# Value products of an attention in one session behind the last transposes, panel parts between the groups of transposes

## The reference, cut to what matters

```
s = einsum('bnqhgd,bnkhd->bnhgqk', qb, kw) * 64 ** -0.5      # 128 queries x 256 keys
s = where(valid, s, -inf)
m = maximum(max(s), sink);  p = exp(s - m)
o = einsum('bnhgqk,bnkhd->bnqhgd', p / (sum(p) + exp(sink - m)), vw)
```

## Time and profile before

| | |
|---|---|
| median of 3 runs | 2661.06 us (2658.98 to 2664.81) |
| the profiled execution, its own time | 2658.54 us |
| its span | 2656.7 us, granted clock 0.992 |
| the four blocks of the first stage | about 70 to 949 us |
| instructions | 39316 |

### The profile page before, as it was taken

One profiled execution on the slowest core, in us unless ns is written; L12 is line 12 of the kernel. 1 busy time (PEld: TensorE's weight loads), 2 busy tenths in 40 slices (PEclk: granted clock), 3 DMA queues, 4 the chain that ended last, 5 costly groups with the idle time before them and its releaser, 6 DMA issues.

```text
span 2656.7 us, 39316 instructions
## 1 busy us (share of the span) xinstructions
PE 2548.2 (96%) x13654; PEld 2054.7 (77%) x13654; DVE 1731.6 (65%) x3010; ACT 1142.4 (43%) x2171; POOL 901.1 (34%) x1018
## 2 busy tenths in 40 slices
PE   7998999999999999989998999999999999999999
PEld 5776777777777777868776888888888888888887
DVE  6678568657756746565656776787666354556665
ACT  5465455555555545644655322342223233322331
POOL 1333100000000046346424766747666222222222
PEclk9999999999999999999999999999999999999999
DMA  4432433343243243164224244323334953445664
GB/s 183 145 112 96 170 103 112 129 144 104 94 179 120 84 187 118 56 230 175 72 90 164 95 147 167 127 96 116 107 129 165 307 172 103 143 131 145 212 184 145
DMA packets 184509, 369.17 MB, mean 139 GB/s; under 512 B 13168, under 2 KB 79088, under 8 KB 181616
## 3 DMA queue, kind: packets, MB, share of 16 engines
q1 hardware_dynamic: 179152, 357.08, 40.3%
q10 hardware_dynamic: 5152, 9.51, 1.0%
HBM read 286.71 MB, written 79.82 MB: 138 GB/s over the span
## 4 chain that ended last, share of the span: by engine, by line
PE 69%; DVE 10%; issue 7%; POOL 5%; ACT 5%; DMA 2%; ACTq 0%; DVEq 0%; SPq 0%; POOLq 0%
PE bank L3260 8%; PE bank L3258 8%; PE bank L3262 8%; PE bank L1567 5%; PE bank L1557 5%; PE bank L1560 5%; PE bank L3238 4%; PE bank L3235 4%; PE bank L3234 4%; PE bank L2188 3%; PE bank L2183 3%; PE bank L2184 3%; POOL m_xlo L2727 2%; POOL wlo L2727 2%; PE bank L1640 2%
## 5 line engine op out<-in xcount | busy, mean ns | idle before, releaser
L478 POOL TENSOR_TENSOR wlo<-raw,whi 128x256 fp32r<-128x256 f32 x372 | 322.7, 899 | 1088.6 <-ACT whi L1162 620.9
L1557 PE MATMUL bank<-hi,whi 128*128 128x512 f32 x704 | 292.2, 415 | 1.6 <-ACT whi L1158 1.6
L1560 PE MATMUL bank<-lo,whi 128*128 128x512 f32 x704 | 278.1, 395 | 5.4 <-DVE lo L1311 5.4
L3262 PE MATMUL bank<-hi,wlo 128*128 128x512 f32 x896 | 275.8, 389 | 0.0
L3258 PE MATMUL bank<-hi,whi 128*128 128x512 f32 x896 | 275.8, 389 | 0.0
L3260 PE MATMUL bank<-lo,whi 128*128 128x512 f32 x896 | 275.8, 389 | 0.0
L3050 DVE TENSOR_TENSOR lo<-h,hi 128x1024 fp32r<-128x1024 f32 x80 | 124.9, 1562 | 172.4 <-ACT hi L2814 172.4
L2745 POOL TENSOR_TENSOR wlo<-h,whi 128x256 fp32r<-128x256 f32 x160 | 128.5, 824 | 297.5 <-ACT whi L2806 297.5
L2183 PE MATMUL bank<-hi,whi 128*128 128x512 f32 x504 | 207.6, 412 | 10.7 <-DVE h L2076 6.4
L2184 PE MATMUL bank<-lo,whi 128*128 128x512 f32 x504 | 196.9, 391 | 0.0
L3262 PEld LDWEIGHTS bank<-hi,wlo 128*128 128x128 f32 x896 | 168.2, 188 | 34.9
(11 more groups left out here) (395 smaller groups left out, 5693.7 us busy)
## 6 DMA issues: line engine op xcount, KB each, us to landing
h<-hidden_scratch SPq DMA_DIRECT2D x96, 512.0 KB, 4.3
raw<-w_mix SPq DMA_DIRECT2D x88, 512.0 KB, 4.0
raw<-w_cross SPq DMA_DIRECT2D x64, 512.0 KB, 3.3
raw<-w_mlp SPq DMA_DIRECT2D x64, 512.0 KB, 4.6
wlo<-mixer_lows_scratch SPq DMA_DIRECT2D x60, 512.0 KB, 3.5
hidden_scratch<-hT SPq DMA_DIRECT2D x116, 256.0 KB, 2.0
h<-w_mlp SPq DMA_DIRECT2D x112, 256.0 KB, 3.0
mixer_lows_scratch<-wlo SPq DMA_DIRECT2D x22, 512.0 KB, 2.9
```

Of the source, the lines that this page charges most:

```text
L478: last = pool.tensor_tensor(wlo[:, i, cols], raw[:, i, cols], whi[:, i, cols].bitcast(F32), ALU.subtract)
L1557: pe.matmul(out, w, hi[:, k, :], start=k == 0, stop=False)
L1560: pe.matmul(out, w, lo[:, k, :], start=False, stop=False)
L3262: last = pe.matmul(down_bank(i)[:], wl[:, cols], xh[:, i % 2, :], start=False, stop=K == KD - 1)
```

## The change

The value products of the four query tiles of an attention are all issued at the last `pv` step (16 matmuls), and `PLACES["pair"]` has other places for the parts of the panels, with a list of its own, `"pair 0"`, for the attention t = 0. Arithmetic, buffers, signals and their counts stay.

```diff
-    "pair": (0, 1, 3, 4, 4, 6, 6, 8, 10, 12),
+    "pair 0": (0, 1, 3, 4, 4, 6, 8, 10, 11, 12),
+    "pair": (0, 1, 3, 4, 6, 8, 10, 12, 13, 14),
@@
-        attention = weave(attention, panels(...), PLACES["pair"])
+        attention = weave(attention, panels(...), PLACES["pair" if h > 1 else "pair 0"])
@@
                     elif kind == "pv":
                         a = step[1]
                         t, q = ATT[a]
-                        if q % 2 == 0:
+                        if q < QT - 1:
                             continue
-                        if q == 1:
-                            pe.wait_ge(h_y.sem, h_y.at(blk, t))
+                        pe.wait_ge(h_y.sem, h_y.at(blk, t))
                         pe.wait_ge(a_pt.sem, a_pt.at(blk, a))
-                        for tq in (q - 1, q):
+                        for tq in range(QT):
                             for kt in range(2):
                                 for odd in range(2):
                                     last = pe.matmul(OUT[odd * SW_D:(odd + 1) * SW_D, tq * P:(tq + 1) * P],
                                                      vsw[:, tq + kt, t // 2 * SW_D:(t // 2 + 1) * SW_D],
-                                                     pT[:, q - 1 + odd, (2 * kt + tq - q + 1) * P:(2 * kt + tq - q + 2) * P],
+                                                     pT[:, tq // 2 * 2 + odd, (2 * kt + tq % 2) * P:(2 * kt + tq % 2 + 1) * P],
                                                      start=kt == 0, stop=kt == 1)
-                                    if tq == q and kt:
+                                    if tq % 2 and kt:
                                         last.then_inc(a_o.sem, 1)
```

More of the change, by code:

```diff
@@ L214, in mixer_steps @@
         attention = weave(attend(h - 1), hg_tail(h - 1) if h > 1 else [], PLACES["tail"])
-        attention = weave(attention, panels(("hg_v", h), ("hg_g", h), ("sw_q", h) if h < NEXT else ("sw_k", h)), PLACES["pair"])
+        attention = weave(attention, panels(("hg_v", h), ("hg_g", h), ("sw_q", h) if h < NEXT else ("sw_k", h)), PLACES["pair" if h > 1 else "pair 0"])
         attention = weave(attention, gates(h)[2:], PLACES["gates"])
```

## The result

The changed kernel takes 2684.12 us in the median (2679.42 to 2689.05, 4 runs), the kernel before 2660.02 beside it (2655.61 to 2664.81, 4 runs): a ratio of 1.0087, 95% interval 1.0074 to 1.0100. The forecast was 2686, slower.

What follows compares the result with a forecast made beforehand. PE, busy 96%, was taken to bound the kernel, but the moved transposes to wait for a DVE and ACT chain: +18.8 us, plus 5.9 for the clock, on 2658.54, plus 2.52 to the median: 2685.8 us, range 2666 to 2699.

Steps and rivals of the forecast that it cites:

- What PE saves if nothing makes it wait: PE, from an attention's first transposes to the next head's: a gain of at most 0.95 us for each attention.
- The working of S: For t > 0, third scores end (S) 4.97 after hg_end's start (H), the next head's transposes come at 16.7.
- The sum: All attentions and the heads behind them: 5.9 + 10.7 + 7.2 - 3.6 - 1.4 = +18.8 us, clock aside.
- The first block: Its attentions: 17.0 us instead of 16.7 from hg_end's start for t > 0; t = 0 slower by 1.5.
- The heads behind t = 2: PE waits there for ACT and DVE as it is: 0.9 us given back four times, -3.6.
- The last attention: Last block, no panels between: the first value products no longer cover the third group's copy, +0.7 us.
- The clock: Falls after a third of the waits added to eleven attentions, 1.6 us each: +5.9, bounds 0 and 17.6.
- the second rival: The clock falls in every one of the eleven attentions with added waits: +36 us, 2697; chance 0.12.
- The signs: Products wait nearly none, transposes 25 to 30 us; DVE's root wait grows 1.1 per attention of t > 0.
- The first rival: PE's saving stands and the chain over DVE and ACT keeps up in the attentions: 2646 us; chance 0.07.

Runs made afterwards that it cites:

- end_late: The whole change, with join 2 before the third scores and hg_end behind the fourth group's scale for t > 0: 2649.45 us, ratio 0.9956 against the kernel before.
- join2_first: The whole change, with join 2 ahead of hg_end on DVE for t > 0: 2667.29 us, ratio 1.0020 against the kernel before.
- filled: The whole change, with spare matmuls on PE ahead of the second group's transposes in eleven attentions: 2680.24 us, ratio 1.0067 against the kernel before.

## Why the prediction was right, point by point

**What PE saves if nothing makes it wait** was right: 0.95 was said, and from hg_end to the transposes the attentions t = 0 of blocks two to four lost 1.05, 1.11 and 1.07 (27.64 to 26.59, 27.65 to 26.54, 27.47 to 26.40). `end_late` shows 1.0 per attention for t > 0 too.

**The working of S** was right link by link. From H: 4.97 to the end of `scores` was said, 4.87 measured (420.51 to 425.38); 2.10 on to the second group's transposes, 2.03; 5.06 to the third's, 4.97 (430.35); 11.7 to the next head, 11.56; H + 16.7 in all, and 16.43 to 16.45 in three of the eight outside the first block, those in which the clock stayed up: 0.26 less each, 2 us for the eight. The heads behind t = 1 and t = 3 kept their lengths within 0.05 us. That join 2 would stand behind the wait was right, and `join2_first` priced it.

**The sum** was right in total, and four of its terms were mis-sized:
- The first block. Its t = 0 lost 1.75 where 1.5 was said. The other three attentions cost 2.7, 3.6 and 4.7 (11.0) where 6.0 was said. I took 17.0 for all; there were 17.85, 18.51 and 19.57. The trace shows PE idle for up to 6.27 at one wait, and `join2_first` takes 7.5 us off these three. I had added 0.3 for hg_end beside POOL and nothing for join 2 behind it, which is 1.1 longer there: 17.85, not 17.0, before the clock.
- The heads behind t = 2 gave back 1.1, 3.9 and 2.5 in the first three blocks and took 2.6 more in the last: 4.9 net where 3.6 was said. Some of it is the clock, which had been low in these heads before as well: from the end of t = 2 to the next attention's first transposes 0.89 before and 0.96 after in block two, but 0.96 in both in block three, where 2.5 came back all the same; 0.80 before and 0.70 after in the last, where the head became longer.
- The last attention cost 3.2 (9.75 to 12.92) instead of 0.7; the copy was right (0.78), the clock was not in that term: 0.79 from 962 to 978, 1.00 in the same attention before.
- The clock. 5.9 was said for a third of eleven attentions at 1.6. It fell in five of eight outside the first block, at 0.9 each, 4.5, and in two of the first block, at 0.65 and 1.7: 6.9 together, near the 5.9 because two errors cancel. A fall cost less than my row said (perhaps since part of it passes while PE waits), and came twice as often. The mean clock went from 0.992 to 0.984, just under the bound that was named as the sign of the second rival; but seven of the eleven had a fall, not eleven, and the rival's 2697 wasn't reached: the sign was set too near.

Between the two profiles the end of the first stage moved by 28.4 (949.31 to 977.75). Of that 1.4 came before 81 us, ahead of every step that was changed, and 2.2 more came behind the stage, where nothing was changed either. 24.7 was forecast and 24.1 is the difference of the medians. Part of that nearness is luck: the three attentions of the first block and the last attention cost 7.4 more than their terms, the eight others with all of the clock's 5.9 cost 3.3 less than theirs, the heads gave back 1.3 more, and the profiles stand 6.4 us further apart than the medians.

**The signs.** The products wait 0.8, DVE's wait grows by 1.1 each, and t = 0 of block two is 1.05 shorter, as said. The transposes wait 40.1, not 25 to 30, 16.6 of it in the first block, in pieces of 1.6 to 6.3 at the second group; and from hg_end to the next head 16.5 to 17 was said, 16.43 to 19.57 came.

**The first rival** (PE's saving stands) fell: it needed hg_end's wait gone. `end_late` took hg_end and join 3 out of the way and got it, 2649 where the rival's price was 2646. By the Trainium skill ("Perfetto Trace Analysis", section "Identifying the Most-Contended Engine") the busiest engine comes first, for TensorE judged by its weight loads rather than its matmuls; PE at 96%, with weight loads at 77% against DVE's 65%, was that engine, and shortening its list lost 24 us until DVE's list was put in order.

**The second rival** had its mechanism shown and its size not. The Trainium skill ("TensorE: Matmul & The Clock Gate", section "HAM oscillation — how this bites in real kernels") has waits between bursts throttle the burst behind them; the trace agrees in seven attentions of eleven, and in `filled`, where PE is kept at work, the clock is 1.00 from the first transposes on in all eleven.

Left open: why DVE's instructions run longer in the first block. POOL is busy for 3.7 us between hg_end and the end of `scores` in each of its three attentions (6.25 to 6.29 us) and not at all in the other blocks (4.88); that POOL is the cause was read from this, not tried by taking POOL's work away. Why the heads behind t = 2 give back what they do was not tried either.

## What to carry to other kernels

When steps of the busiest engine are moved, read what the moved steps had been covering: two parts taken from ahead of a wait and put behind it cost twice, once as idle time and once as work behind the end of the chain. Work it out from the last fixed point of the slower chain (here the start of hg_end), and ask of everything ahead of the chain's next link whether anyone needs it yet; the gain was in DVE steps that nobody waited for yet. Put two moves that need each other in one trial: the new places without the new order on DVE lost 24 us here, the new order without the places 15.

## What the runs showed of the hardware that was not expected

A wait of 2 to 3 us on PE can cost more than itself, by 0.9 us in blocks two to four when the clock falls (17.35 against 16.44). It doesn't fall each time: in these blocks of the changed kernel it fell within 1.2 us behind both waits of 3.38 us, behind three of four of 2.10, and behind neither of 1.59; in the first block during those of 6.27 and 4.46, not at the one of 3.01. Spare matmuls in the wait kept it at 1.00 in all five attentions where it had fallen. In the last attention of `end_late`, with three waits in a row, the sixteen products ran at the lower clock throughout (mean 0.51), 3.58 us instead of 1.90.

The same DVE copy of 128x256 took 0.82 us at 189.73, while POOL was busy, and 0.29 in the second block, where it wasn't; the join around it took 2.17 instead of 1.10.
